# RMS norms over 512 tokens: sums of squares with the tokens on the partitions, one column per 128 tokens, then a diagonal and a ones matmul to spread the reciprocal

## What is computed

```python
def rmsnorm(x, g):
    xf = x.astype(jnp.float32)
    y = xf * lax.rsqrt(jnp.mean(xf * xf, axis=-1, keepdims=True) + NORM_EPS)
    return (y * g.astype(jnp.float32)).astype(x.dtype)

# in each layer of the first block
z = split_columns((rmsnorm(x, pre_g) * (1 + scale) + shift) @ w_in)
q = (rmsnorm(zz['mla_q'], q_norm) @ w_uq)       # mean over 256
kv = (rmsnorm(zz['mla_kv'], kv_norm) @ w_ukv)   # mean over 128
...
x = x + gate * rmsnorm(merged @ w_out, post_g)  # mean over 1024
xc = xc + gate_c * rmsnorm(out_c, post_g)       # layer 0 alone
```

## Time and profile before

| | |
|---|---|
| median of 3 runs | 1541.55 us (1541.48 to 1547.95) |
| the profiled execution | 1542.76 us, its span 1541.0 us |
| PE busy | 1376.8 us (89%) |
| DVE, ACT, POOL busy | 846.5, 639.2, 733.2 us |
| mean granted TensorE clock | 0.958 |

### The profile page before, as it was taken

The page is one execution under the profiler, slowest core; times in us unless marked ns, Lnnn a source line. Parts: engine busy times, 40 slices in busy tenths (PEclk is TensorE's granted clock), DMA queues, the critical chain, the costliest instruction groups (busy, mean ns, idle before and its releaser), DMA issues.

```text
span 1541.0 us, 24544 instructions
## 1 busy us (share of the span) xinstructions
PE 1376.8 (89%) x10288; PEld 1153.1 (75%) x10288; DVE 846.5 (55%) x1213; ACT 639.2 (41%) x1004; POOL 733.2 (48%) x512
## 2 busy tenths in 40 slices
PE   5798899999999999698899899978799888799997
PEld 1654688777777787383787789968688777799996
DVE  2567515431424340657577557479898644598801
ACT  3535322433322323446334554747421123555542
POOL 0520044323212644050696758738644204499983
PEclk8899999999989999799999999989899999999998
DMA  8320123244334432030334335525222134266552
GB/s 340 121 68 14 41 87 101 101 172 142 137 111 175 150 96 82 28 122 16 111 122 137 110 111 157 157 96 177 71 86 71 53 97 124 96 181 189 179 178 82
DMA packets 49118, 180.79 MB, mean 117 GB/s; under 512 B 5488, under 2 KB 6512, under 8 KB 48624
## 3 DMA queue, kind: packets, MB, share of 16 engines
q1 hardware_dynamic: 48864, 177.13, 35.6%
q10 hardware_dynamic: 144, 2.10, 0.3%
HBM read 178.16 MB, written 1.05 MB: 116 GB/s over the span
## 4 chain that ended last, share of the span: by engine, by line
PE 67%; DVE 19%; ACT 5%; DMA 4%; issue 3%; POOL 2%; SPq 0%; ACTq 0%; DVEq 0%
PE ps L368 17%; PE ps L370 16%; PE ps L369 16%; PE ps L372 16%; DMA panels<-weights 3%; DVE work L1838 2%; POOL panels_r L412 1%; ACT panels_hi L402 1%; POOL panels_r L413 1%; PE ps L959 1%; DVE work L1280 1%; DMA const_sb<-constants 1%; DVE small L1007 1%; DVE work_r L1283 1%; DVE work L802 1%
## 5 line engine op out<-in xcount | busy, mean ns | idle before, releaser
L412 POOL TENSOR_TENSOR panels_r<-panels,panels_hi 128x512 fp32r<-128x512 f32 x254 | 373.0, 1468 | 787.1 <-ACT panels_hi L402 785.7
L369 PE MATMUL ps<-h_sb_r,panels_hi 128*128 128x256 f32 (+1 forms) x1408 | 452.0, 321 | 0.0
L402 ACT ACTIVATE panels_hi<-panels 128x1024 fp32r<-128x1024 f32 x254 | 267.5, 1057 | 412.1 <-PE ps L370 236.0
L413 POOL TENSOR_TENSOR panels_r<-panels,panels_hi 128x512 fp32r<-128x512 f32 x254 | 373.4, 1470 | 0.0
L368 PE MATMUL ps<-hi_sb_r,panels_hi 128*128 128x512 f32 (+1 forms) x784 | 278.6, 355 | 27.9 <-DVE h_sb_r L683 14.0
L369 PEld LDWEIGHTS ps<-h_sb_r,panels_hi 128*128 128x128 f32 x1408 | 275.7, 196 | 17.7 <-issue 0.7
L370 PE MATMUL ps<-hi_sb_r,panels_r 128*128 128x512 f32 (+1 forms) x784 | 272.9, 348 | 0.0
L368 PE MATMUL ps<-h_sb_r,panels_hi 128*128 128x256 f32 x624 | 183.6, 294 | 12.3 <-DVE h_sb_r L664 7.6
L368 PE MATMUL ps<-work_r,panels_hi 128*128 128x256 f32 (+1 forms) x560 | 182.7, 326 | 11.7 <-POOL panels_r L413 7.6
L368 PEld LDWEIGHTS ps<-hi_sb_r,panels_hi 128*128 128x128 f32 x784 | 152.9, 195 | 53.6 <-DVE h_sb_r L683 15.3
L370 PE MATMUL ps<-h_sb_r,panels_r 128*128 128x256 f32 x624 | 178.9, 287 | 0.0
(11 more groups left out here) (325 smaller groups left out, 1814.7 us busy)
## 6 DMA issues: line engine op xcount, KB each, us to landing
panels<-weights SPq DMA_DIRECT2D x328, 512.0 KB, 3.6
x_sb<-x_in SPq DMA_DIRECT2D x1, 2048.0 KB, 8.5
x_sb<-x_in ACTq DMA_DIRECT2D x1, 2048.0 KB, 9.6
const_sb<-constants SPq DMA_DIRECT2D x1, 1216.0 KB, 11.0
out<-x_sb SPq DMA_DIRECT2D x2, 512.0 KB, 3.1
vec_sb<-vectors SPq DMA_DIRECT2D x1, 725.0 KB, 12.3
small<-c_in SPq DMA_DIRECT2D x1, 8.0 KB, 1.8
```

Of the source, the lines that this page charges most:

```text
L369: pe.matmul(o, lhsT.hi, rhs.lo, start=False, stop=False)
L402: act.activation(panels_hi[:, m:m + PANEL * P], panels[:, n:n + PANEL * P], ACT.Copy).then_inc(panel_rounded, 1)
L412: pool.tensor_tensor(panels_r[:, at:at + half], panels[:, at:at + half], panels_hi[:, m:m + half], ALU.subtract)
L413: pool.tensor_tensor(panels_r[:, at + half:at + 2 * half], panels[:, at + half:at + 2 * half], panels_hi[:, m + half:m + 2 * half], ALU.su ...
```

## The change

For norms over 512 tokens the squares change sides. A block of squares (128 features x 128 tokens) becomes the stationary operand, and one column of ones is the moving one, so the sums for 128 tokens land on 128 partitions in one column of PSUM; 512 tokens are 4 columns. The root and the reciprocal then work on 128 x 4. To bring the reciprocals back to every partition, DVE multiplies an identity by them (one 128 x 128 diagonal per column), and PE multiplies that by a block of ones into a PSUM bank, from which DVE's multiplies read the reciprocal directly. A class `ByToken` does this in `residual` and in `norm` when T is 512, which is the out part of layer 0 and the norm after it. The first norm of all (`add is None`) and all those over 256 tokens stay as they were. The norm of the latents changes in both layers: 12 one-column products in layer 0 and 8 in layer 1, 2 small roots (8 and 6 columns in all), one small reciprocal, a diagonal of 1024 or 768 columns, and two spreading products, which stand in PE's order after one more gate tile.

```diff
@@ -685,10 +685,39 @@
 
+        class ByToken:
+
+
+            def __init__(self, T, at, sum_bank, spread_bank):
+                self.n, self.sums, self.spread_to = T // P, ps[:, sum_bank, 0:T // P], ps[:, spread_bank, 0:T]
+                self.root, self.inverse = region(work, at, self.n), region(work, at + 8, self.n)
+                self.diagonal = region(work, at + T, self.n, P)
+                (self.diag, self.d0), (self.spread, self.s0) = shared("gla_norm_diag", 1), shared("gla_norm_spread", 1)
+
+            def square_product(self, pe, sq, first, last, signal):
+                for n in range(self.n):
+                    blocks.product(pe, self.sums[:, n:n + 1], sq[:, n * P:(n + 1) * P], const("ones")[:, 0:1],
+                                   first and n == 0, last and n == self.n - 1,
+                                   signal if last and n == self.n - 1 else None)
+
+            def invert(self, dve):
+                steps["dve"](dve.reciprocal(self.inverse, self.root))
+                dve.tensor_tensor(self.diagonal, each(const("ident"), self.n), wide(self.inverse, P), ALU.mult).then_inc(self.diag, 1)
+
+            def spread_product(self, pe):
+                pe.wait_ge(self.diag, self.d0 + 1)
+                blocks.product(pe, self.spread_to, const("ones"), self.diagonal.rearrange("p t n -> p (t n)"), True, True, self.spread)
+
+            def ready(self, dve):
+                dve.wait_ge(self.spread, self.s0 + 1)
+
         def norm(T, x, h, split, scale, at, add=None, between=Stage(), midway=None):
...
             sq, root, inverse = region(work, at, KD, T), region(work, at + KD * T, T), region(work, at + KD * T + T, T)
+            tokens = ByToken(T, at + KD * T, 0, 5) if add is not None and T == TOK else None
+            if tokens is not None:
+                inverse = tokens.spread_to
             order = [5, 6, 7, 0, 1, 2, 3, 4]
@@ -702,8 +731,13 @@
                     pe.wait_ge(squared, q0 + i + 1)
-                    blocks.product(pe, ps[:, 0, 0:T], const("ones"), sq[:, m, :], i == 0, i == KD - 1,
-                                   summed if i == KD - 1 else None)
+                    if tokens is not None:
+                        tokens.square_product(pe, sq[:, m, :], i == 0, i == KD - 1, summed)
+                    else:
+                        blocks.product(pe, ps[:, 0, 0:T], const("ones"), sq[:, m, :], i == 0, i == KD - 1,
+                                       summed if i == KD - 1 else None)
+                if tokens is not None:
+                    tokens.spread_product(pe)
                 if between.tensor is not None:
@@ -715,7 +749,8 @@
                 act.wait_ge(summed, s0 + 1)
-                act.activation(root, ps[:, 0, 0:T], ACT.Sqrt, bias=eps_col[:, 0:1], scale=1.0 / D).then_inc(rooted, 1)
+                of, sums = (root, ps[:, 0, 0:T]) if tokens is None else (tokens.root, tokens.sums)
+                act.activation(of, sums, ACT.Sqrt, bias=eps_col[:, 0:1], scale=1.0 / D).then_inc(rooted, 1)
                 if between.scalar is not None:
@@ -738,7 +773,11 @@
                 dve.wait_ge(rooted, r0 + 1)
-                step(dve.reciprocal(inverse, root))
+                if tokens is not None:
+                    tokens.invert(dve)
+                    tokens.ready(dve)
+                else:
+                    step(dve.reciprocal(inverse, root))
                 if between.vector is not None:
@@ -760,13 +799,20 @@
             total = (bank0 + 6) % 8
+            tokens = ByToken(T, at + 2 * KD * T, total, (bank0 + 7) % 8) if T == TOK else None
+            if tokens is not None:
+                inverse = tokens.spread_to
 
...
                 pe.wait_ge(by_act, a0 + m + 1)
-                blocks.product(pe, ps[:, total, 0:T], const("ones"), sq[:, m, :], m == 0, m == KD - 1, summed if m == KD - 1 else None)
+                if tokens is not None:
+                    tokens.square_product(pe, sq[:, m, :], m == 0, m == KD - 1, summed)
+                else:
+                    blocks.product(pe, ps[:, total, 0:T], const("ones"), sq[:, m, :], m == 0, m == KD - 1,
+                                   summed if m == KD - 1 else None)
 
@@ -795,11 +843,16 @@
                 act.wait_ge(summed, s0 + 1)
-                act.activation(root, ps[:, total, 0:T], ACT.Sqrt, bias=eps_col[:, 0:1], scale=1.0 / D).then_inc(rooted, 1)
+                of, sums = (root, ps[:, total, 0:T]) if tokens is None else (tokens.root, tokens.sums)
+                act.activation(of, sums, ACT.Sqrt, bias=eps_col[:, 0:1], scale=1.0 / D).then_inc(rooted, 1)
 
...
                 dve.wait_ge(rooted, r0 + 1)
-                steps["dve"](dve.reciprocal(inverse, root))
+                if tokens is not None:
+                    tokens.invert(dve)
+                    tokens.ready(dve)
+                else:
+                    steps["dve"](dve.reciprocal(inverse, root))
             return o, inverse, Stage(tensor, scalar, vector, None)
@@ -839,6 +892,9 @@
             (lat_scaled, lc0), (front_taken, fk0) = shared("latent_scaled", 1), shared("front_taken", 4)
+            (lat_diag, ld0), (lat_spread, lp0) = shared("gla_norm_diag", 1), shared("gla_norm_spread", 1)
+            nq = TQ // P
+            lat_root, lat_inverse, lat_wide = root[:, 0:nq + 4], root[:, 16:20 + nq], inverse
 
@@ -857,10 +913,16 @@
                 pe.wait_ge(lat_squared, lq0 + 3)
-                blocks.product(pe, ps[:, 1, 0:TQ], const("ones"), sq_of[0], True, False)
-                blocks.product(pe, ps[:, 1, 0:TQ], const("ones"), sq_of[1], False, True)
-                blocks.product(pe, ps[:, 3, 0:TOK], const("ones"), sq_of[2], True, True, lat_summed)
-                gate_products(pe, early, 4)
+                for i in range(nq + 4):
+                    for j, sq in enumerate((sq_of[0], sq_of[1]) if i < nq else (sq_of[2],)):
+                        c = (i if i < nq else i - nq) * P
+                        blocks.product(pe, ps[:, 1, i:i + 1], sq[:, c:c + P], const("ones")[:, 0:1], j == 0, i >= nq or j == 1,
+                                       lat_summed if i == nq + 3 else None)
+                gate_products(pe, early, early + 1)
+                pe.wait_ge(lat_diag, ld0 + 1)
+                blocks.product(pe, ps[:, 1, 0:TQ], const("ones"), lat_wide[:, 0:TQ], True, True)
+                blocks.product(pe, ps[:, 3, 0:TOK], const("ones"), lat_wide[:, TQ:TQ + TOK], True, True, lat_spread)
+                gate_products(pe, early + 1, 4)
 
@@ -871,8 +933,8 @@
                 act.wait_ge(lat_summed, ls0 + 1)
-                act.activation(root[:, 0:TQ], ps[:, 1, 0:TQ], ACT.Sqrt, bias=eps_col[:, 0:1], scale=1.0 / 256)
-                act.activation(root[:, TQ:TQ + TOK], ps[:, 3, 0:TOK], ACT.Sqrt, bias=eps_col[:, 0:1],
+                act.activation(lat_root[:, 0:nq], ps[:, 1, 0:nq], ACT.Sqrt, bias=eps_col[:, 0:1], scale=1.0 / 256)
+                act.activation(lat_root[:, nq:nq + 4], ps[:, 1, nq:nq + 4], ACT.Sqrt, bias=eps_col[:, 0:1],
                                scale=1.0 / 128).then_inc(lat_rooted, 1)
@@ -885,11 +947,14 @@
                 dve.wait_ge(lat_squared, lq0 + 3)
-                steps["dve"](dve.reciprocal(inverse[:, 0:TQ + TOK], root[:, 0:TQ + TOK]))
+                steps["dve"](dve.reciprocal(lat_inverse, lat_root))
+                dve.tensor_tensor(lat_wide[:, 0:TQ + TOK].rearrange("p (t n) -> p t n", n=P), each(const("ident"), nq + 4),
+                                  wide(lat_inverse, P), ALU.mult).then_inc(lat_diag, 1)
+                dve.wait_ge(lat_spread, lp0 + 1)
                 for m in range(2):
-                    dve.scalar_tensor_tensor(zq[:, m, :], zq[:, m, :], vec(f"q_norm{l}")[:, m:m + 1], inverse[:, 0:TQ],
+                    dve.scalar_tensor_tensor(zq[:, m, :], zq[:, m, :], vec(f"q_norm{l}")[:, m:m + 1], ps[:, 1, 0:TQ],
                                              ALU.mult, ALU.mult)
-                dve.scalar_tensor_tensor(zkv[:, 0, :], zkv[:, 0, :], vec(f"kv_norm{l}"), inverse[:, TQ:TQ + TOK],
+                dve.scalar_tensor_tensor(zkv[:, 0, :], zkv[:, 0, :], vec(f"kv_norm{l}"), ps[:, 3, 0:TOK],
                                          ALU.mult, ALU.mult).then_inc(lat_scaled, 1)
```

## The result

The changed kernel takes 1548.58 us in the median of 15 runs (1545.08 to 1553.56); the kernel before took 1542.42 beside it (15 runs, 1538.14 to 1549.71). The ratio is 1.0035 with a 95% interval of 1.0022 to 1.0047, or 5.4 us more (0.0035 x 1542.4; the interval is 3.4 to 7.2 us, and the medians differ by 6.2). The forecast was 1546.9 us, 5.3 more than before, in a range of 1541.0 to 1550.5. The profiled execution took 1550.61 us, its span 1548.8.

What follows compares the result with a forecast made beforehand. The chain was taken as 67% PE and 19% DVE, with PE bounding layer 0's front. Terms 1.8 + 0.3 + 2.3 + 0.9 = 5.3 us gave 1548.1 profiled, 1546.9 us as median; range 1541.0 to 1550.5.

Steps and rivals of the forecast that it cites:

- Front of layer 0: Layer 0's front, bound by PE: 1.84 us more PE work lost in full, removed reciprocal worth nothing; +1.8 us.
- rival 1: Clock also falls in layer 0's front after 24 one-column records, losing 1.7 us of PE: 1548.6 us; chance 0.22.
- Out part: Out part of layer 0: seven tiles' squares on PE's path, 0.04 us more each; +0.3 us.
- Rival 3: Clock falls between layer 0's out-part tiles, 1.7 us per fall: 1550.3 us with two, 1553.7 with four; chance 0.10.
- First inverse: End of layer 0, root to DVE's first multiply: DVE starts at 628.0 in place of 629.54, 1.5 us early.
- PSUM operands: DVE multiplies reading the reciprocal from PSUM: nothing added by the trace row; 0.5 us more by the skill's errata.
- Squares: Norm between the layers: all 8 tiles of one-column products at half clock, 14.4 us in place of 9.84.
- the lower end: Lower price for the norm's squares at half clock: scaling by 1.72 in place of doubling, giving 12.4 us.
- Rival 2: One-column products do raise the clock among the norm's squares; h 2.3 us early: 1542.3 us; chance 0.17.
- Second inverse: After the norm's squares, up to h: 3.4 us with the spread at half clock, against 4.1 before.
- the three terms together: Both inverses and the norm's squares at the end of layer 0: h starts later, +2.3 us.
- Front of layer 1: Layer 1's front: spread delays gate tile 3, a panel, ACT's rounding and last Silu, which releases `up_tensor`; +0.9 us.

Runs made afterwards that it cites:

- the doubled run: Changed kernel with the latents' sums of layer 0's front made twice over, 48 one-column records in a row; 34.44 us from rotary multiply to up products.
- wide ones in the norm: Changed kernel with 128 columns of ones in place of one in the norm between the layers; 1541.22 us, ratio 0.9991 to the kernel before.
- the fronts alone: Changed kernel with out part and norm between the layers as before, only the two fronts new; 1545.28 us, ratio 1.0014 to the kernel before.
- the last kernel: Changed kernel with layer 0's front as before, 128 columns of ones in norm and out part, layer 1's spread after the last gate tile; 1539.48 us, ratio 0.9968.
- the move of the spread: Kernel with 128 columns of ones in the norm, layer 1's spreading products moved behind the last gate tile; 1542.22 us, ratio 0.9991 to the kernel before.

## Why the prediction was right, point by point

- **Front of layer 0, +1.8.** Right: 1.9 us in each of the executions without a fall of the clock (26.9 to 27.0 for 25.06). In the changed kernel's profile rival 1 came on top, with 1.6 us (predicted 1.7). Rival 1 is the forecast with this fall added, and both occur: the clock fell behind the 24 records in one profile of four, and it fell in the doubled run.
- **Out part, +0.3.** Right. These are the chains of a tile, after and then before:

```profile
607.21 0.79 PE ps L372 x8
607.99 0.35 PE ps L368
```

```profile
610.00 0.86 PE ps L372 x2
610.86 0.23 PE ps L368
```

  A tile's eight records and the first pair record behind them take 1.14 us, where two records and the pair record took 1.09: 0.05 for each tile, where 0.04 had been estimated. Rival 3 did not appear.
- **First inverse, 1.5 early.** Wrong in size: 0.65 us. Root, reciprocal and diagonal took about what the GLA rows gave: the spread began 1.33 us after the root, 1.53 had been taken. The spread was the mis-sized term: 2.09 us and not 0.95 + 0.15, for the clock was at 0.50 when it ran. I had placed the fall inside it, from the earlier trace rows; it came before, with the last tile's squares (0.61 granted in the mean from 628 to 630). The half-clock price was too low as well: a spread that stands alone took 2.09 us at 0.50 and 1.14 at 1.00, not 1.72 and 0.86. This moves between executions: 1.67 with wide ones in the norm, 1.12 in the last kernel.
- **PSUM operands, 0.** Right. The group of the same multiply after (ns min/median/max), to be held against the earlier trace rows:

```profile
L768 DVE TENSOR_TENSOR work<-work,ps x8: 681/681/689, 632.6 to 640.4; 128x512 f32<-128x512 f32 x8
```

  The median with an operand in PSUM is 681 ns, the mean without was 681. The estimate of 0.5 us that was worked out from the Trainium skill ("VectorE: DVE Perf Modes", errata section) did not come about.
- **Squares, 14.4 us.** Right in kind: no clock above 0.50 from the first to the last. Measured 13.83, 0.216 us a record, so the doubled price was the nearer end. (The row behind the lower end holds four records, which are two products and not four; the factor of 1.72 is the same.) Rival 2 is refuted, and with it my reading of the Trainium skill ("TensorE: Matmul & The Clock Gate", Part 1): it says that the gate follows how busy PE has been, and that a stream of loads would count as busy was my inference.
- **Second inverse, 3.4.** Measured 3.39, with a spread of 2.09 where 1.87 was taken and smaller steps before it. For the three terms together h starts 6.29 us later while the table load starts 3.70 later, 2.6 us; with the out part apart the forecast was +2.3.
- **Front of layer 1, +0.9.** Right: 0.84, and 0.85 with the fronts alone. Its mechanism was shown by the move of the spread. DVE's scaling was done 7.7 us after the sums' start, as forecast.

The sum of 5.3 against 5.4 measured is better than its terms, and part of that is luck. 0.9 too much was hoped for from the first inverse and 0.6 too much taken for the squares, and the clock's fall in the first front was left out. The terms as measured in the profiles give 1.9 + 0.35 + 2.6 + 0.84 = 5.7 us without that fall and 7.3 with it. Two bounds were also loose. The lowest values of the terms add up to 1543.9 and not 1544.5, and the range that was said to leave out rival 3 holds its smaller cases (1548.6 and 1550.3). What stays open is how often the clock falls in the first front, and so how much of the 5.4 us it makes: one profile in four is all there is. The stream of squares at half clock came in each of its four profiles.

## What to carry to other kernels

In these traces a float32 record took 0.43 us with 512 moving columns, 0.115 with 128 and 0.1125 with one, so to turn the operands of a float32 reduction shortened nothing: four products with one column took 0.90 us, one with 512 columns 0.86. What it did change is the granted clock. Behind an idle PE, 64 records of one column ran at 0.50 throughout, and the same with 128 columns of ones cost nothing more a record and came back to 1.00. And before a product goes between two tiles, look at which weight panel the later tile frees: here the rounding that waits for that panel's DMA, and the Silu queued behind it, moved by 1.4 us with it. Where the clock has a part, look at the same stretch in several profiles before one of them is called typical.

## What the runs showed of the hardware that was not expected

- 48 one-column records took 7.40 us and the clock stayed at 0.50 for some 10 us; 48 records of 128 columns took 5.52 us at 1.00. PE was busy without a gap in both.
- A record of a float32 product costs 0.115 us with 128 columns (5.52 / 48) and 0.1125 with one at full clock; at half clock one column costs 0.216 us (13.83 / 64).
- Runs of 8 one-column records every 6.39 us among pair products left the clock at 1.00 in every profile, and so did 16 in a row (1.84 us). With 24 in a row (2.7 us) it fell to 0.50 in one profile of four, with 32 (3.6 us) in twelve of thirteen.
